# Mixer units: head norms by logarithm and exponential between two query operations, the last gate job beside the state chain, the first gate's banks freed by a copy

## Chip, cores and metric

One core of a Trainium2 chip runs the kernel. The metric is the device time of one execution in microseconds; less is better. Times below are of one profiled execution unless they are called a median.

## What is computed

Two layers of a streaming encoder, for 512 prompt frames and 32 sample frames together (T = 544 columns). The first layer mixes by two kinds of gated linear recurrence, four HGRN2 heads ("a", 128 key rows each) and four GLA heads ("b", 64 key rows each); the second layer attends. All the change lies in the first mixer:

```python
def gated_linear_recurrence(q, k, v, log_a, s0):     # in blocks of frames
    def step(s, blk):
        qc, kc, vc, ac = blk
        b = jnp.cumsum(ac, axis=1)
        q_dec = qc * jnp.exp(b)
        att = jnp.einsum('blhk,bmhk->bhlm', q_dec, kc * jnp.exp(-b))
        att = jnp.where(causal, att, 0.0)
        o = jnp.einsum('blhk,bhkv->blhv', q_dec, s) + jnp.einsum('bhlm,bmhv->blhv', att, vc)
        s_new = jnp.exp(b[:, -1])[..., None] * s + jnp.einsum('blhk,blhv->bhkv', kc * jnp.exp(b[:, -1:] - b), vc)
        return s_new, o
# ab_mixer, per head:
o_a = rmsnorm(o_a, a_gnorm) * jax.nn.silu(a_g)       # rmsnorm: x * rsqrt(mean(x*x) + eps) * g
o_b = rmsnorm(o_b, b_gnorm) * jax.nn.silu(b_g)
return jnp.einsum('bte,ed->btd', concat(o_a, o_b), w_out)
```

## The kernel before

Activations lie transposed (features on partitions, 544 frame columns as two halves of 272 in two PSUM banks). Weights come from HBM as chunks of 128 x 1024 through four slots; ScalarE copies each to `w_hi` (L699), GpSimd makes the rest `w_lo` (L617), and TensorE multiplies in three passes. One such product over a chunk is a **job** (L1179). The queues of all engines are written out by hand, and semaphores order them. An engine works its queue in order, so a wait holds all that is queued behind it.

The mixer runs over six **units** u: two "b" units with two heads each (e = 0, 1), then four "a" units with one head. For unit u TensorE does `turn_and_score` (transposes of the keys, L1505, and scores, L1491), the key job of unit u+1, `updates` (block products of keys and values, L1518), the query job of unit u+1, `outputs` (products with scores and values, L1549, then with the states, L1558), and per head a gate job and `turn_outputs` (transposes of the normed head, L1570). VectorE runs the chain of the sixteen states (L2125, one step after another), decays and keys of the next unit, the query operations (`queries`: query times its decay, then L2088 and L2096), the head norm (L2144 reciprocals, L2150, L2151), the gate multiply (L2102), and `head_gate` (L2161), `head_lo` (L2172). ScalarE has the gate sigmoids (L861), the decays' Exp (L842 to L846), squares and root of the norm (`head_out`, L889 to L894), `head_hi` (L900), and issues the DMAs that write the final states (L879). `ahead(c)` on ScalarE copies weight chunk c + 2; it is queued right behind the norm's root, in `out_gate`.

PSUM banks 0 to 3 serve the jobs in two pairs. `order` lists all users; user j takes pair j % 2, and it waits until user j - 2 has freed it. The second gate of a unit follows the first with one user between them, and the scores of the second head (or, behind the second "b" unit, the next key job) follow the second gate in the same way. Banks 4 to 7 hold scores, block updates and outputs; `obank(e)` and `OWN` say which.

In the last unit the gate job takes the place of the next key job, and parts of the first jobs of the output projection (`C_O0` to `C_O0 + 2`, over the seven heads that are ready) fill the places of query and gate job.

## Time and profile before

| | us |
|---|---|
| median of 3 runs | 1391.91 (1390.61 to 1395.27) |
| the profiled execution | 1391.11 |
| its span in the profile | 1389.2 |
| TensorE busy | 1374.3 (99%) |
| VectorE, ScalarE, GpSimd busy | 586.2, 559.6, 593.1 |

The granted TensorE clock is full in all of the span (2.4 GHz). The mixer's units lie between 80 and 270 us. As TensorE has work for almost the whole span, an idle time of another engine tells nothing by itself; what counts is where TensorE stands still, and how long before TensorE each chain of the others ends.

### The profile page before, as it was taken

What the parts mean: (1) busy time and instruction counts of PE and PEld (TensorE: products, weight loads), DVE (VectorE), ACT (ScalarE), POOL (GpSimd) and SP (SyncE); (2) the same over time, 40 slices, a digit from 0 to 9 for tenths busy, and PEclk for the clock granted to TensorE, in tenths of its full rate; (3) what the DMA queues carried; (4) which work ended last, traced back from release to release, by engine and by line L of the source; (5) the groups of instructions that cost most, each with busy time, mean ns of one, the idle gap of its engine ahead of it and who ended that gap; (6) DMA issues with size and microseconds to landing.
All of it is one profiled execution on the core that took longest, in us unless ns stands there. A gap on an engine that the chain in (4) does not pass through costs nothing.

```text
span 1389.2 us, 27274 instructions
## 1 busy us (share of the span) xinstructions
PE 1374.3 (99%) x11018; PEld 1296.2 (93%) x11022; DVE 586.2 (42%) x1072; ACT 559.6 (40%) x907; POOL 593.1 (43%) x310
## 2 busy tenths in 40 slices
PE   9999999999999999999999999999999999999998
PEld 7878899999999999999988788878999999999998
DVE  5645566554321332123425966765622122211334
ACT  6546666443421333122454354444533224321223
POOL 5322223326343435334444376564344434443442
PEclk9999999999999999999999999999999999999999
DMA  5232222423342233322332332211223322332221
GB/s 174 89 92 60 56 66 69 117 68 94 95 116 76 76 91 106 90 62 72 89 91 74 83 102 64 55 32 37 86 79 88 107 76 76 90 108 75 83 69 65
DMA packets 206118, 114.39 MB, mean 82 GB/s; under 512 B 16548, under 2 KB 200792, under 8 KB 206040
## 3 DMA queue, kind: packets, MB, share of 16 engines
q1 hardware_dynamic: 200640, 109.39, 27.7%
q10 hardware_dynamic: 5400, 3.89, 0.9%
q8 instruction: 58, 0.95, 0.3%
q14 instruction: 20, 0.16, 0.0%
HBM read 107.30 MB, written 5.96 MB: 82 GB/s over the span
## 4 chain that ended last, share of the span: by engine, by line
PE 95%; DVE 3%; issue 1%; ACT 1%; ACTq 0%; DVEq 0%; POOL 0%; POOLq 0%
PE ps L1179 70%; PE ps L1362 3%; PE ps L1437 3%; PE ps L1377 2%; PE ps L1391 2%; PE ps L1407 2%; PE ps L1701 2%; PE ps L1251 2%; DVE arena L2125 2%; PE ps L1745 2%; PE ps L1713 1%; PE ps L1491 1%; PE ps L1549 1%; PE ps L1518 1%; PE ps L1234 1%
## 5 line engine op out<-in xcount | busy, mean ns | idle before, releaser
L617 POOL TENSOR_TENSOR w_lo<-w_raw,w_hi 128x1024 fp32r<-128x1024 f32 x197 | 489.5, 2488 | 689.3 <-ACT w_hi L699 689.3
L1179 PE MATMUL ps<-x_hi,w_hi 128*128 128x272 f32 x1792 | 373.3, 289 | 2.4 <-DVE arena L2102 2.0
L1179 PE MATMUL ps<-x_hi,w_lo 128*128 128x272 f32 x1792 | 370.8, 288 | 0.0
L1179 PE MATMUL ps<-x_lo,w_hi 128*128 128x272 f32 x1792 | 369.4, 288 | 0.0
L1179 PEld LDWEIGHTS ps<-x_hi,w_hi 128*128 128x128 f32 x1792 | 281.5, 188 | 6.7 <-issue 5.8
L1179 PEld LDWEIGHTS ps<-x_lo,w_hi 128*128 128x128 f32 x1792 | 281.6, 189 | 0.0
L1179 PEld LDWEIGHTS ps<-x_hi,w_lo 128*128 128x128 f32 x1792 | 279.7, 189 | 0.0
L699 ACT ACTIVATE w_hi<-w_raw 128x1024 fp32r<-128x1024 f32 x201 | 210.4, 1051 | 156.1 <-PE ps L1179 138.5
L1179 PE MATMUL ps<-o_hi,w_hi 128*128 128x272 f32 x864 | 179.3, 289 | 0.2 <-DVE xT L1967 0.2
L1179 PE MATMUL ps<-o_hi,w_lo 128*128 128x272 f32 x864 | 178.8, 288 | 0.0
L1179 PE MATMUL ps<-o_lo,w_hi 128*128 128x272 f32 x864 | 178.2, 288 | 0.0
L1179 PEld LDWEIGHTS ps<-o_hi,w_hi 128*128 128x128 f32 x864 | 135.8, 188 | 0.8 <-issue 0.7
L1179 PEld LDWEIGHTS ps<-o_lo,w_hi 128*128 128x128 f32 x864 | 135.8, 188 | 0.0
L1179 PEld LDWEIGHTS ps<-o_hi,w_lo 128*128 128x128 f32 x864 | 134.9, 189 | 0.0
L794 ACT ACTIVATE o_hi<-arena 128x544 f32 x44 | 29.0, 659 | 197.6 <-DVE arena L2005 197.6
L1998 DVE TENSOR_TENSOR arena<-ps,rstd 128x544 f32<-128x544 f32 x44 | 31.9, 725 | 158.6 <-PE ps L1179 150.3
L790 ACT ACTIVATE arena<-arena 128x544 f32<-128x544 f32 x44 | 29.0, 660 | 169.1 <-DVE arena L1998 169.0
L2020 DVE TENSOR_TENSOR xT<-ps,xT 128x544 f32 x32 | 23.2, 725 | 162.9 <-PE ps L1179 162.9
L2005 DVE TENSOR_TENSOR arena<-arena,ps 128x544 f32<-128x544 f32 x44 | 31.7, 722 | 124.3 <-PE ps L1179 123.7
L591 POOL TENSOR_SCALAR arena<-arena,small 128x384 f32<-128x384 f32 (+4 forms) x50 | 53.9, 1090 | 58.5 <-DVE small L2336 58.5
L2008 DVE TENSOR_TENSOR o_lo<-arena,o_hi 128x544 f32 x44 | 33.1, 753 | 42.5 <-ACT o_hi L794 42.5
L2000 DVE TENSOR_TENSOR arena<-arena 128x544 f32<-128x544 f32 x44 | 33.9, 771 | 37.3 <-ACT arena L790 37.3
(332 smaller groups left out, 1728.2 us busy)
## 6 DMA issues: line engine op xcount, KB each, us to landing
w_raw<-in_ffn_w_in SPq DMA_DIRECT2D x88, 512.0 KB, 3.8
w_raw<-in_ffn_w_out SPq DMA_DIRECT2D x32, 512.0 KB, 3.7
w_raw<-in_ab_w_in SPq DMA_DIRECT2D x28, 512.0 KB, 3.9
w_raw<-in_cd_w_in SPq DMA_DIRECT2D x13, 512.0 KB, 4.0
w_raw<-in_ffn_w_out SPq DMA_DIRECT2D x16, 384.0 KB, 3.3
w_raw<-in_ab_w_out SPq DMA_DIRECT2D x8, 512.0 KB, 4.2
arena<-in_x_prompt SPq DMA_DIRECT2D x4, 512.0 KB, 7.7
w_raw<-in_cd_w_in SPq DMA_DIRECT2D x8, 256.0 KB, 5.4
```

Source lines behind the costliest of these rows:

```text
L591: ins = pool.tensor_scalar(p_, p_, rec[:, x % 4, j:j + 1], None, ALU.mult)
L617: pool.tensor_tensor(wl[:, s, :], raw[:, s, :], wh[:, s, :].bitcast(F32), ALU.subtract).then_inc(lo_done, 1)
L699: act.activation(wh[:, s, :], raw[:, s, :], ACT.Copy).then_inc(hi_done, 1)
L790: act.activation(fsig[:, k // 2, :], fg[:, k // 2, :], ACT.Sigmoid).then_inc(f_sig, 1)
L794: act.activation(oh[:, bass.ds(i * 2 + k // 2, 1), :], fh[:, k // 2:k // 2 + 1, :], ACT.Copy).then_inc(f_hi, 1)
L1179: mm = pe.matmul(ps[0:M, b + h, 0:HALF], w[:, s, k * M:(k + 1) * M], xs[x][:, k, h * HALF:(h + 1) * HALF], start=(begin and k == ks[0] and ...
L1362: mm = pe.matmul(ps[:, 7, 0:HALF], w[:, c % SLOTS, k * P:(k + 1) * P], (xh, xl)[x][:, k, h * HALF:(h + 1) * HALF], start=(k == 0 and a == ...
L1437: mm = pe.matmul(ps[:, 4 + i, 0:N], (xh, xl)[x][:, k, i * P:(i + 1) * P], w[:, s, kk * N:(kk + 1) * N], start=(k == 0 and a == 0), stop=(k ...
L1998: dve.tensor_tensor(two(fgk), pair(g), two(rstd[:, :]), ALU.mult).then_inc(frees(g), 1)
L2000: dve.tensor_tensor(fgk, fgk, fsig[:, k, :], ALU.mult).then_inc(f_mul, 1)
L2005: dve.tensor_tensor(two(fh[:, k, :]), two(fgk), pair(u), ALU.mult).then_inc(frees(u), 1)
L2008: dve.tensor_tensor(ol[:, hid, :], fh[:, k:k + 1, :], oh[:, hid, :].bitcast(F32), ALU.subtract)\
```

## The change

Seven edits, all in the mixer.

1. The head norm's factor is made by Ln and Exp(-0.5 x) on ScalarE, with a wait between them, in place of Sqrt there and reciprocals on VectorE.
2. `queries` is cut in two: the norm of head 0 stands between the query product and the decays (`decayed_queries`).
3. In units with two heads the first gate is copied from PSUM by VectorE, which frees its banks; ScalarE's sigmoid and the multiply then work on the copy.
4. In these units ScalarE does the squares and root of head 1 before it issues the state DMAs, and VectorE norms head 1 before `head_lo` of head 0.
5. The keys of the second "b" unit are copied from PSUM by ScalarE, and VectorE multiplies in SBUF.
6. `outputs` starts its first products two state steps earlier, with the last state's update behind them; `obank` and `OWN` are swapped to suit.
7. In the last unit the first job of the output projection and the gate job change places, in TensorE's queue and in `order`; the gate multiply moves behind the states on VectorE.

```diff
--- before.py
+++ after.py
@@ -221,6 +221,9 @@
     at_f1 = order.index(C_F[1])
     order[at_f1:at_f1] = [("o1", m) for m in range(KT)]
     order.insert(order.index(C_M1), "norm")
+    last_turn = order.index(("turn", NU - 1, 0))
+    order[last_turn], order[last_turn + 1] = order[last_turn + 1], order[last_turn]
+    assert order[last_turn] == C_O0
     jof = {key: j for j, key in enumerate(order)}
     for c0 in (0, C_BV, C_M1, C_CV):
         for c in range(c0 + 1, c0 + 4):
@@ -325,7 +328,7 @@
         fh = arena[:, 2 * T:4 * T].rearrange("p (r t) -> p r t", r=2)
         fg = arena[:, 4 * T:6 * T].rearrange("p (r t) -> p r t", r=2)
 
-        OWN = {C_O0 + 1: 4, C_O0 + 2: 6}
+        OWN = {C_O0 + 1: 6, C_O0 + 2: 4}
 
         def bank(c):
 
@@ -405,7 +408,7 @@
         NW = 5
 
         def obank(e):
-            return 6 - 2 * e
+            return 4 + 2 * e
 
         def last(u):
             return len(c_gates[u]) - 1
@@ -833,6 +836,9 @@
                     ch.link(act.activation(t1, t2, ACT.Abs))
                     ch.link(act.activation(t1, t1, ACT.Exp, scale=-1.0))
                     act.activation(t1, t1, ACT.Ln, bias=ones[:, 0:1]).then_inc(u_act, 1)
+                    if u > 0:
+                        wait_done(act, c0)
+                        act.activation(two(kp[:, u % 2, :]), pair(c0), ACT.Copy).then_inc(frees(c0), 1)
 
             def decays(u):
 
@@ -857,6 +863,10 @@
                 ahead(c)
                 act.activation(small[:, 111:112], eps_c, ACT.Sigmoid)
                 act.wait_ge(o_lo, heads_before[u])
+                if e < last(u):
+                    wait_freed(act, c)
+                    act.activation(gate[:, e, :], t1, ACT.Sigmoid).then_inc(gate_sig, 1)
+                    return
                 wait_done(act, c)
                 act.activation(two(gate[:, e, :]), pair(c), ACT.Sigmoid).then_inc(gate_sig, 1)
 
@@ -891,7 +901,12 @@
                 ch.link(act.activation(osq[0:TS, 0:P], ps[0:TS, ob + 1, 0:P], ACT.Square, accum_out=rss[e][0:TS, NT:NT + 1]))
                 for m, i0, i1 in token_tiles:
                     r = rss[e][0:m, i0:i1]
-                    ins = act.activation(r, r, ACT.Sqrt, bias=eps_c[0:m], scale=1.0 / ADV)
+                    ins = act.activation(r, r, ACT.Ln, bias=eps_c[0:m], scale=1.0 / ADV)
+                    ch.add(ins)
+                act.wait_ge(act_s, ch.n)
+                for m, i0, i1 in token_tiles:
+                    r = rss[e][0:m, i0:i1]
+                    ins = act.activation(r, r, ACT.Exp, scale=-0.5)
                 ins.then_inc(r_ors, 1)
 
             def head_hi(u, e):
@@ -954,9 +969,10 @@
                     out_gate(u, 0)
                     ahead(C_O0 + SLOTS - 1 - LEAD)
                     head_out(u, 0)
+                if last(u):
+                    head_out(u, 1)
                 states(u)
                 if last(u):
-                    head_out(u, 1)
                     head_hi(u, 0)
                     out_gate(u, 1)
             head_hi(NU - 1, last(NU - 1))
@@ -1535,9 +1551,7 @@
 
                 kind, i, hs, s0 = unit(u)
                 base = (NB + 1) * u
-                pe.wait_ge(r_r, base + NB - 3)
-                update(u, NB, ps[:, 4, 0:P]).then_inc(r_w, 1)
-                pe.wait_ge(r_r, base + NB)
+                pe.wait_ge(r_r, base + NB - 2)
                 for e, (ko, kz, vc, hd) in enumerate(hs):
                     ob = obank(e)
                     if e:
@@ -1548,8 +1562,10 @@
                         out = ps[0:n1 - n0, ob + t // NT, t % NT * P:(t % NT + 1) * P]
                         mm = pe.matmul(out, att[0:n1 - n0, e, n0:n1], val[0:n1 - n0, t, vc:vc + ADV],
                                        start=(t % NT == 0), stop=False, skip_group_check=True)
-                    if e:
-
+                    if not e:
+                        pe.wait_ge(r_r, base + NB)
+                        update(u, NB, ps[:, 6, 0:P]).then_inc(r_w, 1)
+                    else:
                         mm.then_inc(r_intra, 1)
                         pe.wait_ge(r_intra, units[u][1] + 1)
                     for n in range(1, NB + 1):
@@ -1584,14 +1600,10 @@
                 if more:
                     key_jobs(u + 1)
                 else:
-                    job(g.pop(0), X0)
+                    heads = [k for k in range(KT) if k not in (unit(u)[2][0][3], unit(u - 1)[2][0][3])] + [unit(u - 1)[2][0][3]]
+                    job(C_O0, (oh, ol), ready=lambda k: pe.wait_ge(o_lo, KT - 2 + int(k == heads[-1])), ks=heads, end=False)
                 updates(u)
-                if more:
-                    job(c_query[u + 1], X0)
-                else:
-
-                    heads = [k for k in range(KT) if k != unit(u)[2][0][3]]
-                    job(C_O0, (oh, ol), ready=lambda k: pe.wait_ge(o_lo, KT - 1), ks=heads, end=False)
+                job(c_query[u + 1] if more else g.pop(0), X0)
                 outputs(u)
                 for e in range(last(u) + 1):
                     if g:
@@ -2075,8 +2087,12 @@
                 else:
                     if u == 0:
                         ch.link(dve.tensor_tensor(t2, t2, rstd, ALU.mult))
-                    wait_done(dve, c_key[u])
-                    dve.tensor_tensor(two(kp[:, u % 2, :]), two(t2), pair(c_key[u]), ALU.mult).then_inc(frees(c_key[u]), 1)
+                    if u == 0:
+                        wait_done(dve, c_key[u])
+                        dve.tensor_tensor(two(kp[:, u % 2, :]), two(t2), pair(c_key[u]), ALU.mult).then_inc(frees(c_key[u]), 1)
+                    else:
+                        wait_freed(dve, c_key[u])
+                        ch.add(dve.tensor_tensor(kp[:, u % 2, :], kp[:, u % 2, :], t2, ALU.mult))
 
             def queries(u):
                 r, cq = u % 2, c_query[u]
@@ -2084,20 +2100,31 @@
                 if units[u][0] == "a":
                     dve.wait_ge(u_act, UA[u] + 2)
                     dve.tensor_tensor(two(qp[:, r, :]), two(t4), pair(cq), ALU.mult).then_inc(frees(cq), 1)
-                    wait_freed(dve, cq)
-                    dve.tensor_tensor(qp[:, r, :], qp[:, r, :], t3, ALU.mult).then_inc(q_decayed, 1)
-                    dve.wait_ge(q_decayed, units[u][1] + 1)
                 else:
                     if u == 0:
                         ch.link(dve.tensor_tensor(t3, t3, rstd, ALU.mult))
                     dve.scalar_tensor_tensor(out=two(qp[:, r, :]), in0=pair(cq), scalar=BDK ** -0.5, in1=two(t3),
                                              op0=ALU.mult, op1=ALU.mult).then_inc(frees(cq), 1)
-                    wait_freed(dve, cq)
+
+            def decayed_queries(u):
+
+                r = u % 2
+                wait_freed(dve, c_query[u])
+                if units[u][0] == "a":
+                    dve.tensor_tensor(qp[:, r, :], qp[:, r, :], t3, ALU.mult).then_inc(q_decayed, 1)
+                    dve.wait_ge(q_decayed, units[u][1] + 1)
                 dve.tensor_tensor(blocks(q2[:, r, :]), blocks(qp[:, r, :]), c3(ex[r]).broadcast_to([P, NB + 1, BLK]), ALU.mult)\
                    .then_inc(u_dve, 1)
 
             def out_gate(u, e):
                 c = c_gates[u][e]
+                if e < last(u):
+                    wait_done(dve, c)
+                    dve.tensor_copy(two(t1), pair(c)).then_inc(frees(c), 1)
+                    wait_freed(dve, c)
+                    dve.wait_ge(gate_sig, heads_before[u] + e + 1)
+                    ch.link(dve.tensor_tensor(gate[:, e, :], gate[:, e, :], t1, ALU.mult))
+                    return
                 dve.wait_ge(gate_sig, heads_before[u] + e + 1)
                 dve.tensor_tensor(two(gate[:, e, :]), two(gate[:, e, :]), pair(c), ALU.mult).then_inc(frees(c), 1)
 
@@ -2128,7 +2155,7 @@
             def final_states(u):
 
                 dve.wait_ge(r_w, NW * u + 5)
-                dve.scalar_tensor_tensor(out=rst[:, NB, :], in0=unit(u)[3], scalar=ex[u % 2][:, NB:NB + 1], in1=ps[:, 4, 0:P],
+                dve.scalar_tensor_tensor(out=rst[:, NB, :], in0=unit(u)[3], scalar=ex[u % 2][:, NB:NB + 1], in1=ps[:, 6, 0:P],
                                          op0=ALU.mult, op1=ALU.add).then_inc(r_r, 1)
                 dve.wait_ge(r_r, (NB + 1) * (u + 1))
                 for n in (NB - 1, NB):
@@ -2139,10 +2166,6 @@
                 h, ob = heads_before[u] + e, obank(e)
                 dve.wait_ge(r_ors, h + 1)
                 dve.wait_ge(r_w, NW * (u + 1))
-                for m, i0, i1 in token_tiles:
-                    r = rss[e][0:m, i0:i1]
-                    ch.add(dve.reciprocal(r, r))
-                dve.wait_ge(dve_s, ch.n)
                 if e:
                     dve.wait_ge(r_ot, h)
                 by_value = lambda ap: ap.rearrange("p (t v) -> p t v", v=ADV)
@@ -2176,6 +2199,7 @@
             decays(0)
             keys(0)
             queries(0)
+            decayed_queries(0)
             first_norm()
             l0, l1 = par[:, prow["lb0"]:prow["lb0"] + 4], par[:, prow["lb1"]:prow["lb1"] + 4]
             ch.link(dve.tensor_tensor(cm[:, 0:4], l0, l1, ALU.max))
@@ -2202,8 +2226,6 @@
                     dve.wait_ge(m0_out, 32 * heads_before[u])
                 if u + 1 < NU:
                     key_gates(u + 1)
-                else:
-                    out_gate(u, 0)
                 states(u)
                 if u + 1 < NU:
                     decays(u + 1)
@@ -2212,13 +2234,15 @@
                     queries(u + 1)
                 else:
                     final_states(u)
+                    out_gate(u, 0)
                 head_norm(u, 0)
                 if u + 1 < NU:
+                    decayed_queries(u + 1)
                     out_gate(u, 0)
                 if last(u):
                     head_gate(u, 0)
+                    head_norm(u, 1)
                     head_lo(u, 0)
-                    head_norm(u, 1)
                     out_gate(u, 1)
             head_gate(NU - 1, last(NU - 1))
             head_lo(NU - 1, last(NU - 1))
```

## Rows read from the trace of the kernel before

**Rows 1.** Windows: us, then busy time of each engine, clock, DMA share, GB/s

```profile
80.00:270.00 190.00, 183.80 (x1775) 170.41 (x1774) 102.76 (x254) 108.70 (x228) 50.54 (x22) 1.00 0.25 72
```

**Rows 2.** Waits of TensorE, summed: us, times, longest us

```profile
PE ps L1179 <- DVE arena L2102: 2.0, 2, 1.0
PE ps L1549 <- DVE arena L2125: 1.8, 3, 0.9
PE ps L1570 <- DVE arena L2151: 1.2, 2, 0.6
...
PE ps L1179 <- DVE arena L2079: 0.4, 1, 0.4
```

**Rows 3.** TensorE in order of time: start, us, engine, line, operation [idle before]

```profile
121.29 2.59 PE L1491 MATMUL ps<-arena 64*128 64x128 f32 x20
...
151.63 0.49 PE L1179 MATMUL ps<-x_hi,w_hi 128*128 128x272 f32 x2 [1.00 <-DVE arena L2102]
...
158.44 0.83 PE L1570 MATMUL ps<-ident,arena 128*128 128x128 f32 x5 [0.56 <-DVE arena L2151]
...
184.19 0.83 PE L1570 MATMUL ps<-ident,arena 128*128 128x128 f32 x5
...
186.72 0.52 PE L1179 MATMUL ps<-x_hi,w_hi 128*128 128x272 f32 x2
...
261.23 0.77 PE L1570 MATMUL ps<-ident,arena 128*128 128x128 f32 x5
```

**Rows 4.** VectorE in order of time, query operation and norms of two units

```profile
182.32 0.72 DVE L2096 TENSOR_TENSOR arena<-arena,small 128x544 f32<-128x544 f32 x1
...
183.20 0.69 DVE L2150 TENSOR_TENSOR arena<-ps,small 128x512 f32<-128x512 f32 x1
183.81 0.33 DVE L2151 TENSOR_SCALAR arena<-ps,small 32x128 f32<-32x128 f32 x1
...
259.60 0.69 DVE L2150 TENSOR_TENSOR arena<-ps,small 128x512 f32<-128x512 f32 x1
```

**Rows 5.** ScalarE in order of time, norm's root in two units

```profile
144.71 1.28 ACT L894 ACT_TABLE_LOAD   x1
...
182.19 0.48 ACT L894 ACTIVATE small<-small 128x4 f32<-128x4 f32 x2
182.58 1.04 ACT L699 ACTIVATE w_hi<-w_raw 128x1024 fp32r<-128x1024 f32 x1
```

**Rows 6.** ScalarE, the first norm: Ln (L761), then Exp (L764)

```profile
33.98 0.38 ACT L761 ACTIVATE rcol<-ps,small 128x4 f32<-128x4 f32 x2
34.38 1.28 ACT L764 ACT_TABLE_LOAD   x1
```

**Rows 7.** GpSimd in order of time, two of the w_lo

```profile
124.41 2.39 POOL L617 TENSOR_TENSOR w_lo<-w_raw,w_hi 128x1024 fp32r<-128x1024 f32 x1 [3.11 <-ACT w_hi L699]
...
183.70 2.36 POOL L617 TENSOR_TENSOR w_lo<-w_raw,w_hi 128x1024 fp32r<-128x1024 f32 x1 [10.14 <-ACT w_hi L699]
```

**Rows 8.** VectorE, head_lo beside the first of these

```profile
124.68 2.70 DVE L2172 TENSOR_TENSOR o_lo<-arena,o_hi 128x544 fp32r<-128x544 f32 x1
```

**Rows 9.** ScalarE and its DMA issues, first unit and last

```profile
111.42 0.62 ACT L861 ACTIVATE arena<-ps 128x544 f32<-128x544 f32 x1 [1.57 <-PE ps L1179]
...
112.67 0.62 ACTq L879 DMA_DIRECT2D out_p_gla<-arena  x1
...
114.04 0.28 ACT L889 ACTIVATE arena<-ps 128x128 f32<-128x128 f32 x1 [1.99 <-issue]
...
117.28 0.64 ACT L900 ACTIVATE o_hi<-arena 128x544 fp32r<-128x544 f32 x1
...
120.29 0.61 ACT L861 ACTIVATE arena<-ps 128x544 f32<-128x544 f32 x1
...
257.54 1.28 ACT L894 ACT_TABLE_LOAD   x1
257.56 0.34 ACTq L879 DMA_DIRECT2D out_p_hgrn<-arena  x1
```

## The prediction

> **What bounds the kernel now.** I read the windows by stage first, then TensorE's waits, then the timelines of the four engines around each of those waits. In the stretch from 80 to 270 us, which holds the recurrent units of the first mixer, TensorE is busy for 183.8 of 190 us at full granted clock [rows 1]. So the mixer is bound by TensorE, and all that an edit there can win is the 6.2 us in which it stands still. The waits name 5.4 us of it: 2.0 for the second gate job of the two "b" units (the multiply L2102 frees the banks), 1.8 ahead of the outputs (the state chain L2125), 1.2 for the norm of the second head (L2151), 0.4 for the keys (L2079) [rows 2]. The other side is the larger one: each chain of VectorE and ScalarE that now ends just ahead of TensorE can be made late. In a unit with one head the transposes of the head (L1570) start at 184.19, with no idle time ahead of them [rows 3], and the norm that feeds them ends at 183.81 + 0.33 = 184.14 [rows 4]. That chain has 0.05 us to spare, and the change lengthens it.
>
> **Part 1, the head norm on ScalarE.** Now a head pays one table load and two small Sqrt operations, which end at 182.67 in this unit [rows 5], and two reciprocals on VectorE. The change writes Ln, a wait for it, then Exp. What a following Exp costs is in the trace: after the Ln of L761 a new load of 1.28 us stands ahead of the Exp of L764 [rows 6]. I take the same here. Ln takes the place of Sqrt at equal price, then 1.28 for the load and about 0.4 for two small Exp (two Sqrt took 0.48 [rows 5]): the norm factor comes at 182.67 + 1.7 = 184.35 instead of 182.67. All that is queued on ScalarE behind it moves by the same 1.7: the weight copy of L699 from 182.58 to 184.3, and with it GpSimd's w_lo, which starts 1.12 behind that copy, from 183.70 to 185.4 [rows 5, 7].
> The Trainium skill (ScalarE: Activation LUTs, section "Table sets: the hidden batching unit") says that Ln followed by Exp needs one load, since one set holds both. The trace does not agree: a load stands between the two [rows 6]. By the Trainium skill's rule the 1.28 us would be absent; rival A works that out.
>
> **Part 2, head norm between the two query operations.** VectorE's order in such a unit is now query product, decay (L2088), second decay (L2096), norm; the scores of the next unit wait for L2096. After the change it is query product, norm, L2088, L2096. The norm waits for 184.35, takes 0.95 (183.20 to 184.14 [rows 4]) and ends at 185.3; the head's transposes start there instead of at 184.19. L2088 follows at 185.25, just ahead of w_lo at 185.4. L2096 meets w_lo. Both its inputs lie in SBUF, and such an operation stood still behind a running w_lo: L2172 began at 124.68, took 2.70 where L2096 of the same size takes 0.72 [rows 4], and ended at 127.38, 0.6 after the w_lo of 124.41 to 126.80 [rows 7, 8]. So w_lo runs either at once (185.4 to 187.8) or behind L2088 (186.0 to 188.35); L2096 ends 0.6 later, at 188.4 to 188.95. I take the later. Now it ends at 183.04 [rows 4].
> The Trainium skill (SBUF — State Buffer, section "Who interferes with whom") says the two engines share a port pair and that the one that starts first keeps it for its whole instruction; the L2172 row fits, and the sum goes by that row.
> TensorE then starts the key transposes at 188.99, and they and the scores take 1.8 (2.53 from 184.19 to 186.72, less 0.77 for the head's own transposes, as at 261.23 [rows 3]). The next job starts at 190.8 instead of 186.72: **+4.0 us in each of the three "a" units that have a successor, 12.1 in sum.** With w_lo first it is 3.5 each. The multiply of the gate and the freeing of its banks end by 189.9, so they hide.
>
> **Part 3, the units with two heads.** The first gate's banks are freed by a copy (0.72, as the other 128x544 operations of VectorE [rows 4]) in place of sigmoid and multiply, the key's banks by ScalarE's copy, which lies in idle time. In the first unit the key wait of 0.4 goes [rows 2], so the first gate job is done at 111.05 instead of 111.42 [rows 9], the copy at 111.75 and the second gate job starts at 111.9. Now it starts at 111.42 + 0.62 + 0.72 and some 0.2 of passing on, 112.95: 1.05 are won, and the turn of the second head by 1.3 in all, since its norm no longer stands behind the DMA issues, though Ln plus Exp still make it 0.35 late. But the second gate's sigmoid is behind more work: it waits in ScalarE's queue for the first sigmoid (now behind the copy, to 112.4), for the squares and Ln (114.04 to 117.36 now [rows 9], so 112.4 to 115.75), and then for four DMA issues of 0.62 [rows 9], which ran beside the first sigmoid before. The issues can run under Exp's load (L879 at 257.56 ran under the load at 257.54 [rows 9]), from 115.75 to 118.3. From there L900 to sigmoid is 3.0 as now (117.28 to 120.29 [rows 9]): sigmoid at 121.3, multiply to 122.7, banks free at 122.8. The scores of the second head of the next unit use those banks and would start at 121.2 (they start 1.26 after the row at 121.29, 122.55, now [rows 3]). So TensorE waits 1.6 there, and the unit ends **0.3 late**. If the issues don't run under the load it ends 1.3 later still.
> In the second such unit the same chain is followed by an "a" unit. State wait gone: 0.2 ahead at its first gate job. The squares are done where the load of 144.71 starts [rows 5], so the norm factor comes at 148.45 and the norm ends at 149.4. L2088 runs to 150.0, w_lo from there to 152.4, L2096 to 153.0, and only then the bank copy, to 153.7: second gate job at 153.8 instead of 151.63 [rows 3]. Then as above: turn of the second head at 160.3 instead of 158.44 [rows 3], DMA issues to 160.2, sigmoid at 163.2, banks free at 164.7 instead of at 161, where the next job starts now. **+3.7 us in sum after both units.**
>
> **Part 4, the state chain.** Outputs may start two state steps earlier, with the extra state's product behind the first intra products. Three waits of 1.8 us in sum, the longest 0.9 [rows 2], are hidden by 1.4 us of products. Two of these lie in units whose end is set by part 2 or 3, where nothing of them is left over but what is counted. In the last unit a full gate job (6.2: 151.63 to 158.44 less the wait of 0.56 [rows 3]) and no multiply ahead of the chain cover it: **-1.0 us**. There the first output job takes the odd bank pair and waits for head_gate of the unit before, at 190.7 in the times of part 2, where TensorE comes at 190.8: nothing, or 0.1.
> At the end of the last unit the head's turn starts at 261.23, after a norm that starts at 259.60 [rows 3, 4]. Norm start plus 1.7 less the 0.25 of reciprocals plus 0.95 gives 262.0: **+0.7 us**.
>
> **Sum:** 3.7 + 12.1 - 1.0 + 0.7 = 15.5 us. The profiled execution took 1391.11 us (span 1389.2), 0.8 under the median of 1391.91. 1391.1 + 15.5 = 1406.6, and against the median 1407.4; I give 1407. Behind the mixer nothing is seen to absorb it: what follows waits for the same TensorE.
>
> **Rivals.**
> A, one table set serves Exp, Ln and Exp. The norm factor then comes at 181.85, and w_lo at 182.9. L2088 still goes first, L2096 is still caught, to 186.5 or so: 1.6 per "a" unit, 4.8; the two-head units leave 1.3, the last gives -1.0: +5.1, 1396.5 to 1397. If the set is loaded with Ln but only Exp is spared, +9.6, 1401. For it: it is the cheapest order of loads. Against it: [rows 6].
> B, L2096 and w_lo don't meet (w_lo comes late, or waits for both decays). Then L2096 ends at 186.7 and a unit loses 1.8: 5.4 + 1.7 - 1.0 + 0.7 = 6.8, some 1398.5. For it: the two starts lie 0.15 us apart at L2088, but L2096 would have to be 0.7 early, so it is unlikely.
> C, worse: in the first unit w_lo starts ahead of the query operation by 0.1 and holds the copy for 2.3 us more, and the issues don't run under the load (1.3 twice): up to 1412.
> D, faster: the change does what it is written as, all the waits of [rows 2] go and nothing new comes. Its point: the norm factor must be there before 182 in the "a" unit and L2096 must end ahead of w_lo, so that it takes rival A in full and no meeting of ports. Then 1391.9 - 5.4 = 1386.5. For it: the waits are there. Against it: [rows 5, 6, 8].
> E, about no change: A without the meeting, but with the late sigmoid in the two-head units, 1391 to 1393.
>
> **How the numbers follow.** Forecast 0.64, A 0.14, B 0.08, C 0.06, D 0.04, E 0.04. About 0.3%, 4.2 us, is what a measurement of this kernel can tell from no change. Forecast, A, B and C are slower by more than that (A's lower end, +4.6, is near it, so I leave 0.02 of A to no change): slower 0.90, same 0.06, faster 0.04. The forecast's own bounds are 3.5 for 4.0 in part 2 (-1.6), Exp of 0.2 to 0.5, and +2.6 for the issues. The range takes in B and half of A: 1398 to 1411.
>
> **What would show it.** ACT_TABLE_LOAD twice per head norm at L894's place (16 in place of 8, eight heads); a VectorE decay operation of over 2 us beside w_lo in each "a" unit; TensorE idle ahead of the head's turn by some 1.2 and ahead of the key transposes by some 2.8 in three units; idle of 1.6 to 1.8 at the scores and at the key job behind the two-head units, released by the gate multiply; no wait for L2125. The prediction is wrong if Exp comes without a load, or if the decay operations keep 0.73 us. A faster kernel would show TensorE's idle time in the mixer under 2 us.

## The result, and the profile after

The changed kernel takes 1414.99 us (median of 6 runs, 1414.48 to 1416.38) against 1392.11 for the kernel before beside it: 1.0161 times as long, 95% interval 1.0147 to 1.0176. Times are medians; this ratio and those below are of the means of the runs, so they differ a little from the quotient of the medians. Two of the ten runs of the kernel with edits 6 and 7 alone took 1797 and 1902 us at a mean granted clock of 0.69 and 0.65, and are left out of its ratio. The direction was forecast; 22.9 us instead of 15.5 was not, and the time lies above the range. The span of the profiled execution grew from 1389.2 to 1413.5, by 24.3.

The stretch of the units in windows of the changed kernel (us, TensorE's busy time and instructions, granted clock, DMA share, GB/s; it ends 22 us later than that of [rows 1]):

```profile
80.00:292.00 212.00, 192.75 (x1775) 0.94 0.23 64
```

TensorE idles for 19.25 us where it idled for 6.2, so 13.05 more, and it is *busy* for 8.95 us more with the same work. That is the whole growth of 22.0 in this stretch. Measured to the same job of the kernel, 8.8 us behind the turn of the last head (270.0 and 292.6), the growth is 22.6: 13.2 of idle time and 9.4 of busy time. The mean granted clock of 0.94 is the sign of the second part. TensorE's waits in the changed kernel (us in total, times, longest), to be set beside [rows 2]:

```profile
PE ps L1521 <- DVE arena L2116: 7.8, 3, 2.6
PE ps L1586 <- DVE arena L2174: 5.2, 5, 1.7
PE ps L1195 <- DVE arena L2123: 3.7, 2, 3.3
PE ps L1507 <- DVE arena L2129: 1.6, 1, 1.6
PE ps L1195 <- POOL w_lo L620: 0.7, 1, 0.7
```

No wait for the state chain is left, and none for the keys. In their place stand the key transposes (L1521, was L1505) behind the decay operation L2116 (was L2096), the turn of a head (L1586, was L1570) behind its norm L2174, and the second gate job (L1195, was L1179) behind the copy L2123. The same in order of time, for TensorE (start, us, line, operation, idle time before and who ended it), where [rows 3] has the rows of before:

```profile
111.96 0.49 PE L1195 MATMUL ps<-x_hi,w_hi 128*128 128x272 f32 x2 [0.34 <-DVE arena L2123]
...
122.82 1.79 PE L1507 MATMUL ps<-arena 64*128 64x128 f32 x10 [1.60 <-DVE arena L2129]
...
156.44 0.49 PE L1195 MATMUL ps<-x_hi,w_hi 128*128 128x272 f32 x2 [3.31 <-DVE arena L2123]
...
167.26 0.49 PE L1195 MATMUL ps<-x_hi,w_hi 128*128 128x272 f32 x2 [0.66 <-POOL w_lo L620]
...
191.58 0.83 PE L1586 MATMUL ps<-ident,arena 128*128 128x128 f32 x5 [1.36 <-DVE arena L2174]
...
195.00 1.27 PE L1521 MATMUL ps<-ident,arena 128*128 128x128 f32 x5 [2.59 <-DVE arena L2116]
...
283.83 0.83 PE L1586 MATMUL ps<-ident,arena 128*128 128x128 f32 x5 [0.58 <-DVE arena L2174]
```

At 195.00 the five key transposes take 1.27 us; the same operation takes 0.76 at 164.77 in the changed kernel. That row holds both parts of the loss: 2.59 us of standing still, and then slow work.

The chain in the first one-head unit, ScalarE first (compare [rows 5]; L904 is Ln, L909 Exp):

```profile
187.17 1.28 ACT L904 ACT_TABLE_LOAD   x1
188.46 0.48 ACT L904 ACTIVATE small<-small 128x4 f32<-128x4 f32 x2
188.96 1.28 ACT L909 ACT_TABLE_LOAD   x1
190.26 0.21 ACT L909 ACTIVATE small<-small 128x4 f32<-128x4 f32 x1
```

then VectorE (compare [rows 4]): norm, first decay, second decay:

```profile
190.59 0.69 DVE L2173 TENSOR_TENSOR arena<-ps,small 128x512 f32<-128x512 f32 x1 [2.80 <-ACT small L909]
191.20 0.33 DVE L2174 TENSOR_SCALAR arena<-ps,small 32x128 f32<-32x128 f32 x1
191.45 0.70 DVE L2114 TENSOR_TENSOR arena<-arena 128x544 f32<-128x544 f32 x1
192.19 2.75 DVE L2116 TENSOR_TENSOR arena<-arena,small 128x544 f32<-128x544 f32 x1
```

and GpSimd:

```profile
191.58 2.79 POOL L620 TENSOR_TENSOR w_lo<-w_raw,w_hi 128x1024 fp32r<-128x1024 f32 x1 [11.75 <-ACT w_hi L702]
```

w_lo starts 0.13 behind L2114, takes 0.4 more than the 2.4 of [rows 7] and ends at 194.37; L2116 ends at 194.94, 0.6 later, as L2172 did in [rows 8]. Lastly the granted clock of the changed kernel around two of the waits, in windows of 2 us:

```profile
121.00:123.00 2.00, 0.40 (x4) 1.00 0.00 0
123.00:125.00 2.00, 2.00 (x12) 0.61 0.67 182
125.00:127.00 2.00, 2.00 (x11) 0.50 0.30 89
127.00:129.00 2.00, 2.00 (x10) 0.50 0.00 0
129.00:131.00 2.00, 2.00 (x13) 0.69 0.71 196
...
256.00:258.00 2.00, 0.72 (x4) 0.64 0.08 25
258.00:260.00 2.00, 2.00 (x11) 0.50 0.77 229
260.00:262.00 2.00, 2.00 (x10) 0.50 0.03 8
262.00:264.00 2.00, 2.00 (x12) 0.66 0.00 0
```

0.50 is 1.2 GHz. TensorE stood still for 1.60 us ahead of 122.82; from 123 to 131 us it is busy without a gap, and for some 7 us of that it has half the clock. There are five such falls, one in each unit but the last. The kernel before has none in this stretch.

### The profile page after: what moved, and what is told of

Read it like the earlier page. It is cut to its first block, busy times and chain, and to the rows that moved or that the text cites. A ratio compares the mean times of both kernels' runs of the same rounds, so it can differ in the third digit from the quotient of the medians.

```text
span 1413.5 us, 27291 instructions
## 1 busy us (share of the span) xinstructions
PE 1385.5 (98%) x11022; PEld 1306.6 (92%) x11022; DVE 602.3 (43%) x1058; ACT 572.2 (40%) x932; POOL 595.0 (42%) x310
## 4 chain that ended last, share of the span: by engine, by line
PE 86%; issue 8%; POOL 2%; DVE 2%; ACT 1%; DMA 0%; ACTq 0%; POOLq 0%; DVEq 0%
PE ps L1195 66%; PE ps L1378 3%; PE ps L1453 3%; POOL w_lo L620 2%; PE ps L1393 2%; PE ps L1407 2%; PE ps L1713 2%; PE ps L1757 1%; PE ps L1725 1%; DVE arena L2116 1%; PE ps L1534 1%; DVE o_lo L1913 1%; PE ps L1507 0%; PE ps L1749 0%; DMA arena<-in_x_prompt 0%
## 5 line engine op out<-in xcount | busy, mean ns | idle before, releaser
L1195 PE MATMUL ps<-x_hi,w_hi 128*128 128x272 f32 x1792 | 375.0, 290 | 4.3 <-DVE arena L2123 3.7
L1195 PE MATMUL ps<-x_hi,w_lo 128*128 128x272 f32 x1792 | 372.5, 289 | 0.0
L1195 PE MATMUL ps<-x_lo,w_hi 128*128 128x272 f32 x1792 | 371.1, 289 | 0.0
L1195 PEld LDWEIGHTS ps<-x_hi,w_hi 128*128 128x128 f32 x1792 | 283.3, 189 | 8.8 <-issue 7.1
L1195 PEld LDWEIGHTS ps<-x_lo,w_hi 128*128 128x128 f32 x1792 | 283.1, 190 | 0.0
L1195 PEld LDWEIGHTS ps<-x_hi,w_lo 128*128 128x128 f32 x1792 | 281.4, 190 | 0.0
L1195 PE MATMUL ps<-o_hi,w_hi 128*128 128x272 f32 x864 | 179.8, 289 | 0.2 <-DVE xT L1979 0.2
L1195 PE MATMUL ps<-o_hi,w_lo 128*128 128x272 f32 x864 | 179.3, 289 | 0.0
L1195 PE MATMUL ps<-o_lo,w_hi 128*128 128x272 f32 x864 | 178.6, 288 | 0.0
L1195 PEld LDWEIGHTS ps<-o_hi,w_hi 128*128 128x128 f32 x864 | 136.4, 189 | 0.8 <-issue 0.5
L1195 PEld LDWEIGHTS ps<-o_lo,w_hi 128*128 128x128 f32 x864 | 136.3, 189 | 0.0
L1195 PEld LDWEIGHTS ps<-o_hi,w_lo 128*128 128x128 f32 x864 | 135.3, 190 | 0.0
```

What stands on the lines that cost most here:

```text
L1195: mm = pe.matmul(ps[0:M, b + h, 0:HALF], w[:, s, k * M:(k + 1) * M], xs[x][:, k, h * HALF:(h + 1) * HALF], start=(begin and k == ks[0] and ...
```

## The experiments

My theory after the result had three parts: (1) Exp's own table load makes every head norm 1.7 us late; (2) the norm ahead of the decays puts them behind that and into w_lo; (3) the idle time so made lets the granted clock fall, which costs again. The rivals: edits 3 to 7 (copies, queues, banks) carry a good part; the slow operations are slow for another reason than ports; the busy time grew for another reason than idle time. All runs, with TensorE's idle and busy time from 80 us to the end of the units (to a whole us, so the busy time is good to some 0.6 us):

| run | ratio to before | 95% interval | idle, us | busy, us | clock falls |
|---|---|---|---|---|---|
| before | 1 | | 6.2 | 183.8 | 0 |
| changed | 1.0161 | 1.0147 to 1.0176 | 19.3 | 192.8 | 5 |
| edit 1 undone | 1.0053 | 1.0034 to 1.0073 | 10.8 | 186.2 | 2 |
| edit 2 undone | 1.0045 | 1.0028 to 1.0063 | 11.6 | 187.4 | 2 |
| edits 1 and 2 undone | 0.9977 | 0.9966 to 0.9989 | 3.4 | 182.6 | 0 |
| weight copy late | 1.0055 | 1.0038 to 1.0071 | 13.2 | 186.8 | 2 |
| idle time filled | 1.0118 | 1.0100 to 1.0137 | 9.3 | 196.7 with the fill | 1 |
| before + edits 6, 7 | 1.0001 | 0.9990 to 1.0011 | 6.3 | 184.8 | 0 |
| before + edit 1 | 1.0091 | 1.0074 to 1.0108 | 12.4 | 188.6 | 1 |
| before + edit 2 | 1.0074 | 1.0057 to 1.0091 | 13.6 | 187.4 | 2 |
| DMA issues late | 1.0145 | 1.0130 to 1.0161 | 17.6 | 192.4 | 5 |
| 1 and 2 undone, issues late | 0.9973 | 0.9963 to 0.9983 | 2.8 | 183.2 | 0 |

### Edit 1 undone: Sqrt and reciprocals again

```diff
-                    ins = act.activation(r, r, ACT.Ln, bias=eps_c[0:m], scale=1.0 / ADV)
-                    ch.add(ins)
-                act.wait_ge(act_s, ch.n)
-                ...
-                    ins = act.activation(r, r, ACT.Exp, scale=-0.5)
+                    ins = act.activation(r, r, ACT.Sqrt, bias=eps_c[0:m], scale=1.0 / ADV)
 # head_norm, VectorE
+                    ch.add(dve.reciprocal(r, r))
```

> The changed kernel with the head norm's root and reciprocals as before (its edit 1 undone), the rest kept. If the Exp and its table load carry the loss, this comes near the time before, 1395 or less. If the place of the norm ahead of the decays and the meeting of L2116 with w_lo carry it, the norm is done 1.4 us earlier in each one-head unit, but w_lo starts earlier with it and still holds a decay operation: some 2.5 us of idle per one-head unit stay, and the time is 1403 to 1408. If edits 3 to 7 carry it, 1412 or more.

1400.08 us, 1.0053: between the first two expectations. The idle time ahead of the turn of a head is nearly gone (0.2 in sum). That ahead of the key transposes is not smaller by anything:

```profile
PE ps L1516 <- DVE arena L2111: 7.8, 3, 2.6
```

VectorE and GpSimd of this kernel in the first one-head unit:

```profile
182.77 0.70 DVE L2109 TENSOR_TENSOR arena<-arena 128x544 f32<-128x544 f32 x1
183.51 2.75 DVE L2111 TENSOR_TENSOR arena<-arena,small 128x544 f32<-128x544 f32 x1
```

```profile
182.65 3.03 POOL L620 TENSOR_TENSOR w_lo<-w_raw,w_hi 128x1024 fp32r<-128x1024 f32 x1 [10.14 <-ACT w_hi L702]
```

The weight copy is queued behind the norm's root, so w_lo comes with it, early or late: without Exp both come earlier and meet all the same.

### Edit 2 undone: decays ahead of the norm

```diff
                     queries(u + 1)
+                    decayed_queries(u + 1)
                 ...
                 head_norm(u, 0)
                 if u + 1 < NU:
-                    decayed_queries(u + 1)
                     out_gate(u, 0)
```

> The changed kernel with both decay operations ahead of the head norm again (edit 2 undone), Ln and Exp kept. If the place of the norm with the port meeting carries most of the loss: idle ahead of the key transposes goes, 1.1 to 1.4 us ahead of the head's turn stay in each one-head unit (the late Exp), the first gate's copy of the second two-head unit is no longer late, and the clock falls in the one-head units go with the idle: 1394 to 1399. If the Exp load carries the loss by itself: 1405 or more.

1399.28, 1.0045. Both decays take 0.72 again and the norm stands behind Exp with VectorE idle (this kernel, first one-head unit):

```profile
184.21 0.72 DVE L2114 TENSOR_TENSOR arena<-arena 128x544 f32<-128x544 f32 x1
184.97 0.72 DVE L2116 TENSOR_TENSOR arena<-arena,small 128x544 f32<-128x544 f32 x1
186.97 0.69 DVE L2173 TENSOR_TENSOR arena<-ps,small 128x512 f32<-128x512 f32 x1 [1.28 <-ACT small L909]
```

No wait of TensorE for L2116 is left. 5.7 us for the norm are, 1.6 at the scores, 1.8 for w_lo behind the second two-head unit, 1.5 put down to "issue", and two clock falls. One of these (216 to 219 us) lies in the one-head units, where I had expected none. The time is 0.3 above the 1394 to 1399 that I expected of the edit order. Exp's load, with what hangs on it, costs about as much as the order does.

### Edits 1 and 2 both undone

Both diffs above together.

> The changed kernel with edits 1 and 2 both undone: only the copied gate banks, the earlier second root, the copied keys, the earlier outputs and the last unit's new order are left. If edits 3 to 7 do what they are written as, TensorE's idle in the mixer is under 2 us (5.6 before) and the time is 1386 to 1389. If they bring a late sigmoid of the second gate also with Sqrt, 1391 to 1394. If they are what slows the kernel, over 1400.

1389.47, ratio 0.9977: under the kernel before, so edits 3 to 7 are not what slows it. No fall of the clock in the stretch. Its waits:

```profile
PE ps L1581 <- DVE arena L2173: 0.8, 3, 0.4
PE ps L1190 <- issue: 0.7, 1, 0.7
PE ps L1190 <- DVE arena L2118: 0.6, 2, 0.3
PE ps L1190 <- POOL w_lo L620: 0.4, 1, 0.4
```

The time is 0.5 above the expected 1386 to 1389, and the idle time is 3.4, not under 2. The 0.7 put down to "issue" stands ahead of the first output job, which now shares its banks with the unit before: head_gate of that unit (L2183) ends at 235.31 and the job starts at 235.41. The wait for w_lo goes with the move of the DMA issues (last run below).

How much edits 3 to 7 win is less sure than that they don't lose. The runs of the kernel before lie in two groups, near 1390.7 and near 1395.2, and the ratio mixes both. All ten runs of this kernel (1388.24 to 1390.18) are below the lowest of the 22 beside them (1390.40), but against the lower group alone the gain is some 0.1%.

### The weight copy behind the sigmoid

```diff
 # out_gate, ScalarE
-                ahead(c)
+                if u + 1 == NU:
+                    ahead(c)
                 ...
                 act.activation(..., ACT.Sigmoid).then_inc(gate_sig, 1)
+                ahead(c)
```

> The changed kernel with one move: the weight copy that stands ahead of each gate sigmoid on ScalarE (and with it GpSimd's w_lo) comes behind the sigmoid, except in the last unit. If w_lo's meeting with the decay operation costs what the trace says, L2116 takes 0.72 instead of 2.75, 2.0 us less per one-head unit and in the second two-head unit, 1 us less for each second gate, and shorter clock falls: 1397 to 1405. If the meeting is only a coincidence of slow operations, L2116 stays at 2.75 and the time at 1413 to 1416.

1401.07, 1.0055. L2119 (L2116 in the changed kernel) now runs free, since w_lo starts after it:

```profile
186.36 0.72 DVE L2119 TENSOR_TENSOR arena<-arena,small 128x544 f32<-128x544 f32 x1
```

```profile
187.77 2.36 POOL L620 TENSOR_TENSOR w_lo<-w_raw,w_hi 128x1024 fp32r<-128x1024 f32 x1 [13.78 <-ACT w_hi L702]
```

The wait ahead of the key transposes went from 2.59 to 0.56 in each of the three units, by 2.03, the 2.75 - 0.72 of the operation. The operation and its data are as in the changed kernel; only w_lo was moved. So the meeting with w_lo is the cause of the 2.75, and it cost 6.1 us of idle time in these units.

### The idle time filled

```diff
+                        if u == 1 and e:
+                            keep_busy(11, 4)
                         job(g.pop(0), X0)
+                        if more and not last(u):
+                            keep_busy(4)
                 ...
                     turn_outputs(u, e)
+                if more and not last(u):
+                    keep_busy(8)
```

> The changed kernel, with products of the identity into a free bank put on TensorE where it stands still: 4 ahead of each one-head unit's turn, 8 ahead of its key transposes, 11 ahead of the second gate job of the second two-head unit. They fill the idle time and move no other engine. If the jobs behind an idle time are slow because the granted clock fell with TensorE idle, the falls of the last four units go (only that behind the late sigmoid stays, where no bank is free) and the time drops by 5 to 7 us to 1407 to 1410, with no wait made shorter. If the slow jobs have another cause (ports, memory), it stays at 1414 to 1416, and if the fill delays real work, it is higher.

`keep_busy(n)` puts n products of the identity into a free bank. 1407.49, 7.5 us under the changed kernel, with no work taken away and products added. Its clock stays full where it fell before (two of its windows around the last wait for a decay operation, and the key transposes behind that wait, which take 0.77 here and 1.33 at 257.28 in the changed kernel):

```profile
254.00:256.00 2.00, 2.00 (x18) 1.00 0.86 260
256.00:258.00 2.00, 2.00 (x18) 1.00 0.01 2
```

```profile
253.66 0.77 PE L1521 MATMUL ps<-ident,arena 128*128 128x128 f32 x5 [0.62 <-DVE arena L2122]
```

The stretch of the units is 206 us instead of 212; 1.7 of the rest is a fall later on (below). Only the fall behind the late sigmoid is left, where nothing was filled in. Not all of the 7.5 us is the fill's. From the second gate job of the second two-head unit, right behind the first fill, to the turn of the last head this kernel takes 121.8 us (155.67 to 277.50) and the changed kernel 127.4 (156.44 to 283.83): 5.6 us. Another 1.5 us lie ahead of any fill, where the fall behind the same wait of 1.60 lasts 4 us (124 to 128) instead of 8 (123 to 131); why it is shorter isn't shown. Where the idle time was filled the four falls are gone, so the slow jobs there are slow because the clock falls after TensorE stood still. One wait grew: the key job behind the second two-head unit waits 1.8 for w_lo instead of 0.7, as the jobs ahead of it are now fast and arrive earlier.

### Each of three edits alone, on the kernel before

Edits 6 and 7 (state chain):

```diff
-                pe.wait_ge(r_r, base + NB - 3)
-                update(u, NB, ps[:, 4, 0:P]).then_inc(r_w, 1)
-                pe.wait_ge(r_r, base + NB)
+                pe.wait_ge(r_r, base + NB - 2)
                 ...
+                    if not e:
+                        pe.wait_ge(r_r, base + NB)
+                        update(u, NB, ps[:, 6, 0:P]).then_inc(r_w, 1)
 # and the swapped banks and the new order of the last unit, as in the change
```

> The kernel before with the state chain edits alone (outputs two steps earlier, last gate job beside the chain, banks swapped). All three waits for L2125 go, 1.8 us, and 0.7 us come back as the first output job waits for the head gate of the unit before: 1 to 1.5 us under the kernel before. If the extra update behind the first products costs what it hides, no change at all.

1393.16, ratio 1.0001: no change. The three waits for the chain are gone, and as much has come elsewhere. Its waits:

```profile
PE ps L1573 <- DVE arena L2150: 2.0, 5, 0.6
PE ps L1182 <- DVE arena L2101: 2.0, 2, 1.0
PE ps L1182 <- DVE arena L2078: 0.9, 1, 0.9
PE ps L1182 <- issue: 0.8, 1, 0.8
```

The wait for the key multiply (0.4 in [rows 2]) is 0.5 longer: counted from the start of the first unit the multiply ends only 0.1 later, so most of it is TensorE coming earlier. The norm holds the turn of the one-head units for 0.2 to 0.4, since TensorE arrives earlier at a chain that had 0.05 us to spare; 0.8 is the shared bank pair (head_gate ends at 239.77, the job starts at 239.87).

Edit 1 alone:

```diff
-                    ins = act.activation(r, r, ACT.Sqrt, bias=eps_c[0:m], scale=1.0 / ADV)
+                    ins = act.activation(r, r, ACT.Ln, bias=eps_c[0:m], scale=1.0 / ADV)
+                    ...
+                    ins = act.activation(r, r, ACT.Exp, scale=-0.5)
-                    ch.add(dve.reciprocal(r, r))
```

> The kernel before with Ln and Exp in the head norm alone. If a second table load is on the path of every head: 1.3 to 1.7 us of idle ahead of each one-head unit's turn and 1.7 more in each two-head unit, some 8 us, and one to two clock falls of 2 us: 1400 to 1405. If the load hides behind the gate job: within 1 us of before.

1403.71, 1.0091: on the path of every head, as the first expectation says, though with 1.0 ahead of each one-head unit's turn instead of 1.3 to 1.7:

```profile
PE ps L1575 <- DVE arena L2152: 7.3, 6, 2.0
PE ps L1184 <- DVE arena L2107: 2.6, 3, 1.3
```

Edit 2 alone, with Sqrt:

```diff
                 head_norm(u, 0)
                 if u + 1 < NU:
+                    decayed_queries(u + 1)
                     out_gate(u, 0)
```

> The kernel before with the norm between the query operations alone, Sqrt kept. If the order and the port meeting cost without Exp too: idle of 2.5 us ahead of the key transposes in each one-head unit, w_lo beside a decay operation of over 2 us, 1400 to 1404. If the order is only harmful because Exp makes the norm late: within 1 us of before.

1403.13, 1.0074, and one wait carries it, ended by the second decay operation beside w_lo:

```profile
PE ps L1505 <- DVE arena L2100: 7.4, 3, 2.5
```

### The DMA issues behind the second sigmoid

```diff
                 if last(u):
                     head_out(u, 1)
-                states(u)
-                if last(u):
                     head_hi(u, 0)
                     out_gate(u, 1)
+                states(u)
```

> The changed kernel with the four DMA issues of the final states moved behind the second gate's sigmoid in the two-head units. If the issues stand on the path of that sigmoid, head_hi starts 1.0 us earlier, where Exp ends, and the wait ahead of the scores (1.60) becomes 0.6; whether the granted clock still falls behind it decides between 1413 (1 us less, fall kept) and 1409 to 1411 (fall at 123 us gone as well). If the issues are not on the path, 1414 to 1416.

1411.64, 3.4 us under the changed kernel. The wait ahead of the scores is 0.52 instead of 1.60, and the clock still falls behind it (0.50 from 124 to 127 us), but is back by 128 instead of by 131. So the issues were on the path of the sigmoid. Of the 3.4 us, 1.1 are this wait, 1.5 the shorter fall behind it, and 0.7 the wait for w_lo behind the second two-head unit, which is gone. I had expected either all of the fall or none of it. That the shorter wait made the fall shorter is not shown: behind the full 1.60 it also lasts only some 4 us in the filled kernel and with edit 2 undone.

The same move with edits 1 and 2 undone:

> The kernel with edits 1 and 2 undone, with the same move of the DMA issues: the two small waits behind the two-head units (0.23 at the scores, 0.39 at the key job) go. 0.3 to 0.8 us less than with edits 1 and 2 undone alone, 1388.5 to 1389.5, and 0.2% to 0.4% under the kernel before. If it is not below 0.998 of before, the gain of edits 3 to 7 is not real.

1388.02 (11 runs) against 1390.85, ratio 0.9973 (0.9963 to 0.9983): the fastest of all kernels here, and 0.5 under the expected range. The two small waits are gone. Against the run without the move the intervals overlap, so what the move itself brings there is not shown. The ratio is below the 0.998 that I had set as the mark of a real gain, though its interval reaches 0.9983.

## Why the prediction was right in its waits and wrong in its time

**Part 1, Exp's load: right.** Eight loads for Ln and eight for Exp. The load is 1.28, the weight copy moved with the norm (w_lo meets the decays), and the turn waits 1.36, 1.70 and 1.35 in the three one-head units. Rival A falls with it. The Trainium skill (ScalarE: Activation LUTs, section "Table sets: the hidden batching unit") has one load for Ln and then Exp; the trace of the changed kernel disagrees again, with the load at 188.96.

**Part 2, order and port: right.** Said: 1.2 ahead of the turn and 2.8 ahead of the key transposes, 4.0 in sum. Found: 3.95, 4.29 and 3.94. L2116 was to take over 2 us and took 2.75. The moved weight copy showed the cause. Rival B gave a price of 1.8 per unit without the meeting; the kernel with the weight copy late shows 1.34 + 0.56 = 1.90 in the first and the third such unit, and 1.69 + 0.56 = 2.25 in the second.

**Part 3, two-head units: right in the first, half right in the second.** First: 1.60 ahead of the scores (said 1.6); the second gate job starts at 111.96 (said 111.9), and the turn of the second head waits 0.23 (said 0.35). Second: 3.31 ahead of the gate job (3.4 by the prediction's times: 153.8 less 150.4, which is 151.63 without its old wait of 1.00 and 0.2 earlier). But the key job behind it waits 0.66 for w_lo, not 1.8 for the gate multiply. The second gate job ran at half clock (156.44 to 164.06, 7.6 us instead of 6.2), and the multiply's chain passed behind it. The filled kernel has the 1.8, put down to w_lo.

**Part 4, state chain: right for this kernel, and only for it.** The waits for it are gone, and the wait for the bank pair of head_gate, put at 0 to 0.1, doesn't show in the changed kernel. But edits 6 and 7 alone bring nothing (1.0001): there that wait is 0.76, with edits 1 and 2 undone 0.75, and with edit 2 undone 1.25. It is hidden only where TensorE comes late. The wait at the end of the last unit is 0.58 (said 0.7).

**The step that failed is the sum.** It added idle times and took each job at its old duration. The idle time alone was near: 15.5 said, 13.2 found. By the waits listed, the one-head units have 11.8 more (12.1 said), the last unit 0.3 less (as said), and the two-head units 2.0 more, where 3.7 was said; there part of the delay is slow work instead of idle time. What the sum had no term for is the granted clock: TensorE's busy time grew by 9.4 us up to the same job, of which 0.4 is only that the first unit begins 0.4 later, so 9.0 in the units; and 1.7 us more went in a fall at 915 us, far behind the mixer (clock 0.57 from 915 to 919). 13.2 + 9.4 + 1.7 = 24.3, the whole growth of the span. The prediction noted the full clock ahead of it [rows 1] and drew nothing from it, and named no rival in which it falls. The filled kernel shows the term: from its first fill to the last turn it takes 5.6 us less, with no work taken away.

**Why the two edits cost more together.** Alone on the edits 3 to 7 (0.9977), edit 1 adds 0.0068 and edit 2 0.0076; together they add 0.0184, so 0.0040, about 5 us, comes from their meeting (5.1 by the medians; the intervals of the ratios reach 0.0012 to 0.0019 to either side, so the size is rough). Five clock falls instead of two fit that, as does the wait of the second two-head unit (3.31, with 1.80 under edit 2 alone and 0.28 under edit 1 alone).

**Left open.** What it takes for the clock to fall isn't settled. With edit 1 undone TensorE waited 2.59 us in each of the three one-head units, and the clock fell only behind the second; with edit 2 alone it waited 2.45 to 2.47, and the clock fell only behind the first two. In the kernel with the weight copy late, three like pairs of waits (1.34 to 1.69, then 0.56) were followed by a fall in the first and the third unit, and by none in the second; with edits 6 and 7 alone 1.0 us did nothing. Falls between 886 and 919 us appear in the profiles of several kernels, one without Exp among them (clock 0.57 from 886 to 894 with edits 1 and 2 undone), and not in others. The two groups of the kernel before differ in their granted clock: over the whole span it is 0.999 to 1.000 in the runs near 1390.7, and 0.997 or 0.998 in most of those near 1395.2. So falls go with the longer time in most of these; where in the span they lie no profile of such a run shows.

## What to carry to other kernels

Where one engine is busy 97% of a stretch, look at each chain of the others for how long before it they end; here the norm's chain had 0.05 us, and work added to such a chain, or any early step given to the busy engine, turned into a wait. Price an idle time of TensorE twice: as itself, and as slower work that may follow it, here 9.0 us on 13.2. The second price isn't due each time, so it is a range and not a number. And before two VectorE operations are moved, look at what GpSimd does at their new place, and at what in another queue is moved along with them.

## What the runs showed of the hardware

- The granted clock can drop to 1.2 GHz behind TensorE's idle time and stay there with TensorE fully busy, for 3 to 8 us (123 to 131 us, 256 to 264). It doesn't do so each time: behind like waits of 2.59 us it fell once in three. Independent products into a free bank kept it at full speed and paid for themselves: 5.6 us less in the stretch that has them.
- A VectorE operation with two SBUF inputs and GpSimd's w_lo hold each other up in both directions: L2116 took 2.75 instead of 0.72, and w_lo 2.79 instead of 2.4 where it started 0.13 behind L2114. With edit 1 undone w_lo took 3.03, although its record starts 0.12 ahead of the first decay, L2109, which kept its 0.70; so the starts in the profile, this close together, don't tell which of the two is held up.
- Table loads come between Ln and Exp each time (1.28 each), and DMA issues on ScalarE's queue run under such a load: here L909's load and the first of the issues in the first unit of the changed kernel.

```profile
115.82 1.28 ACT L909 ACT_TABLE_LOAD   x1
115.84 0.56 ACTq L889 DMA_DIRECT2D out_p_gla<-arena  x1
```
